# The order of the score matmuls of a head pair in a two-layer hybrid decoder: both heads interleaved, or one head after the other

## The reference, cut to what matters

```python
z = jnp.einsum('bhtd,bhsd->bhts', q_blk, k_blk) * scale      # 8 heads, d = 64
strict = s_idx < t_idx
log_beta = jax.nn.log_sigmoid(z)
log_rest = jnp.where(strict, jax.nn.log_sigmoid(-z), 0.0)
rev = lax.cumsum(log_rest, axis=3, reverse=True)
after = jnp.pad(rev[..., 1:], ((0, 0), (0, 0), (0, 0), (0, 1)))
a = jnp.exp(jnp.where(strict, log_beta + after, -jnp.inf))
outs.append(jnp.einsum('bhts,bhse->bhte', a, v_blk))
```

## Time and profile before

| what | us |
|---|---|
| median of 3 runs | 1523.18 |
| the profiled execution, whole | 1523.18 |
| its span, first to last instruction | 1521.4 |
| TensorE busy | 1476.3 (97% of the span) |
| VectorE busy | 1153.8 (76%) |
| ScalarE busy | 1007.6 (66%) |

### The profile page before, as it was taken

The page is one execution under the profiler, slowest core; times in us unless marked ns, Lnnn a source line. Parts: engine busy times, 40 slices in busy tenths (PEclk is TensorE's granted clock), DMA queues, the critical chain, the costliest instruction groups (busy, mean ns, idle before and its releaser), DMA issues.

```text
span 1521.4 us, 20635 instructions
## 1 busy us (share of the span) xinstructions
PE 1476.3 (97%) x7842; PEld 1261.1 (83%) x7842; DVE 1153.8 (76%) x872; ACT 1007.6 (66%) x834; POOL 15.5 (1%) x44
## 2 busy tenths in 40 slices
PE   5999999999999899999999999999999999999997
PEld 5897899997897788888888888888888888888775
DVE  4466544445466588899888888989889988888996
ACT  4577543344677477677777767767777776776775
POOL 3000000000000000000000000000000000000000
PEclk9999999999999899999999999999999999999999
DMA  9442555554443399999989999999999999999993
GB/s 342 146 139 97 180 169 193 178 190 156 139 139 97 111 359 372 370 330 374 374 318 373 377 319 376 371 332 362 376 355 340 377 369 322 374 375 321 348 359 128
DMA packets 185376, 430.75 MB, mean 283 GB/s; under 512 B 9048, under 2 KB 11096, under 8 KB 185328
## 3 DMA queue, kind: packets, MB, share of 16 engines
q1 hardware_dynamic: 181920, 426.27, 78.2%
q0 software_dynamic: 1184, 3.22, 0.6%
q10 hardware_dynamic: 2224, 0.59, 0.2%
HBM read 429.01 MB, written 1.05 MB: 283 GB/s over the span
## 4 chain that ended last, share of the span: by engine, by line
PE 89%; ACT 4%; DVE 3%; issue 1%; DMA 1%; ACTq 0%; DVEq 0%
PE ps L1264 81%; PE ps L1606 2%; PE ps L1636 2%; DMA wif<-in_w_in_dram 1%; ACT whi L454 1%; DVE wlo L835 1%; ACT L464 1%; PE ps L1283 1%; DVE y L857 0%; PE ps L1673 0%; PE ps L1671 0%; PE ps L1425 0%; PE ps L1410 0%; DVE y L1022 0%; ACT qkc L626 0%
## 5 line engine op out<-in xcount | busy, mean ns | idle before, releaser
L835 DVE TENSOR_TENSOR wlo<-raw,whi 128x2048 fp32r<-128x2048 f32 x405 | 926.4, 2291 | 290.3 <-ACT whi L454 289.7
L454 ACT ACTIVATE whi<-raw 128x2048 fp32r<-128x2048 f32 x405 | 776.8, 1919 | 408.0 <-PE ps L1264 406.9
L1264 PE MATMUL ps<-whi,xT_hi 128*128 128x512 f32 x1056 | 418.2, 396 | 1.5 <-DVE wlo L835 1.5
L1264 PE MATMUL ps<-wlo,xT_hi 128*128 128x512 f32 x1056 | 411.8, 390 | 0.0
L1264 PE MATMUL ps<-whi,xT_lo 128*128 128x512 f32 x1056 | 411.1, 389 | 0.0
L1264 PEld LDWEIGHTS ps<-wlo,xT_hi 128*128 128x128 f32 x1056 | 198.3, 188 | 42.5
L1264 PEld LDWEIGHTS ps<-whi,xT_hi 128*128 128x128 f32 x1056 | 198.3, 188 | 40.8 <-issue 1.7
L1264 PEld LDWEIGHTS ps<-whi,xT_lo 128*128 128x128 f32 x1056 | 198.5, 188 | 39.1
L1264 PE MATMUL ps<-whi,hid_hi 128*128 128x512 f32 (+1 forms) x536 | 210.9, 393 | 0.7 <-DVE hid_lo L1150 0.7
L1264 PE MATMUL ps<-wlo,hid_hi 128*128 128x512 f32 (+1 forms) x536 | 208.7, 389 | 0.0
L1264 PE MATMUL ps<-whi,hid_lo 128*128 128x512 f32 (+1 forms) x536 | 208.6, 389 | 0.0
(11 more groups left out here) (218 smaller groups left out, 838.4 us busy)
## 6 DMA issues: line engine op xcount, KB each, us to landing
raw<-in_moe_w_gate_dram SPq DMA_DIRECT2D x112, 1024.0 KB, 5.2
raw<-in_moe_w_up_dram SPq DMA_DIRECT2D x112, 1024.0 KB, 5.4
raw<-in_moe_w_down_dram SPq DMA_DIRECT2D x112, 1024.0 KB, 5.2
raw<-in_w_in_dram SPq DMA_DIRECT2D x28, 1024.0 KB, 5.4
raw<-in_ffn_w_gate_dram SPq DMA_DIRECT2D x10, 1024.0 KB, 5.1
raw<-in_ffn_w_up_dram SPq DMA_DIRECT2D x10, 1024.0 KB, 5.1
raw<-in_ffn_w_down_dram SPq DMA_DIRECT2D x10, 1024.0 KB, 4.9
raw<-in_w_out_dram SPq DMA_DIRECT2D x8, 1024.0 KB, 5.0
```

The source lines that it names most:

```text
L454: act.activation(whi[:, i % NSPLIT, :], raw[:, i % NRAW, :], ACT.Copy).then_inc(hi_ready, 1)
L835: dve.tensor_tensor(wlo[:, i % NSPLIT, :], raw[:, i % NRAW, :], whi[:, i % NSPLIT, :].bitcast(F32), ALU.subtract).then_inc(lo_ready, 1)
L1264: ins = pe.matmul(acc, lhs, rhs, start=start and m == 0, stop=stop and m == 2, skip_group_check=True)
```

## The change

Only `pair_scores` is changed, and in it only the order. Before, each kind of matmul is issued for both heads in turn. After, the four of one head come first, and then the four of the other. The matmuls, their operands, the wait ahead of them and the signal behind the last are the same. The lines behind move up by one.

```diff
                 def pair_scores(p):
                     if p == 0:
                         pe.wait_ge(proj_out, 7 * l + KS + 1)
-                    heads = [(slice(64 * a, 64 * a + 64), ps[:, 4 + a, :]) for a in range(2)]
-                    for s, z in heads:
+                    for a in range(2):
+                        s = slice(64 * a, 64 * a + 64)
+                        z = ps[:, 4 + a, :]
                         pe.matmul(z[:, 0:256], ksT[s, p, 0:P], qsT[s, p, :], start=True, stop=False,
                                   skip_group_check=True)
-                    for s, z in heads:
                         pe.matmul(z[:, 256:384], ksT[s, p, P:], qsT[s, p, P:], start=False,
                                   stop=False, skip_group_check=True)
-                    for s, z in heads:
                         for c in (0, 256):
                             ins = pe.matmul(z[:, c:c + P], ident_b[:], mask_s[:], start=False,
                                             stop=False, skip_group_check=True)
                     ins.then_inc(z_ps, 1)
```

## The result

The changed kernel takes 1531.41 us (median of 4 runs, 1530.53 to 1532.31), the kernel before 1522.60 us beside it (4 runs, 1520.34 to 1525.19). The ratio is 1.0058, with an interval of 1.0043 to 1.0074. Timed again, with five more runs of it beside 22 of the kernel before, the ratio is 1.0047 (1.0033 to 1.0061). The forecast, 1530.6 us or 1.0049 of the median of 1523.18, lies in both intervals, and the measured time in the forecast's range of 1527.0 to 1533.5.

A forecast was written before the change was run, and what follows sets the result against it. TensorE's chain was taken to bound the kernel. Each layer grows 4 x 0.96 - 0.16 = 3.68 us, the kernel 7.4 us: span 1528.8 us, with 1.8 us around it 1530.6 us; range 1527.0 to 1533.5.

The forecast's parts named there:

- What bounds: Whole kernel: TensorE carries 89% of the chain, the pair scores lie on it, and their added time moves everything behind.
- 0.96 us a pair: At each of 8 score pairs: added time, 0.65 us from lost overlap plus 0.31 us from switches.
- the overlap: In a score pair: no pass of one head runs beside one of the other any more, 0.65 us a pair.
- the switches: In a score pair: the array goes from 128 rows to 64 and back twice, not once, 0.31 us a pair.
- What goes back: Third pair's wait before the sums vanishes, 0.16 us a layer; fourth pair's, some 0.4 us, vanishes but gains nothing.
- Loads open: Rival, score pairs: weight load lies open at each of a lone head's four passes, 1.56 us a pair, 1535.4 us; chance 0.05.
- Only the overlap is lost: Rival, score pairs: no switch costs anything more, 0.65 us a pair, 1528.1 us; chance 0.12.
- Absorbed: Rival: the delay falls into later waits or the overlap isn't lost, no change, 1523 us; chance 0.04.
- The clock: Rival: low-clock stretches near 350 to 370 and 500 to 530 us shift into idle, 1520 us or less; chance 0.02.

The follow-up runs named there:

- same rows: Kernel before with both heads of a pair reading partitions 0 to 63, order of instructions unchanged: 1.0030 of before.
- two-switch kernel: Kernel before, heads still in turn, with the masks of the first 128 columns moved between the 256-column and the 128-column scores: 1.0013 of before.
- the kernel with the masks last: Kernel before with each head's two scores issued together, then the other head's, and the four masks behind both: 0.9994 of before.
- groups of 6: Kernel before with each head's scores as three matmuls of 128 columns, all the first head's ahead of the second's, then four masks: 1.0016 of before.
- kernel with narrow matmuls in turn: Kernel before with each head's scores as twelve matmuls of 32 columns (24 passes), the heads alternating, then the four masks: 1546.33 us, one run.
- and by head: Kernel before with twelve 32-column score matmuls (24 passes) a head, all the first head's issued before the second's: 1584.52 us, one run.

## Why the prediction was right, step by step

- **What bounds.** Right. The scores are on the chain, and each 0.1 us at a pair moves the end. The kernels order themselves by the length of a pair, with 8 pairs and 0.3 us that goes back: pairs of 1.37, 1.40, 1.71 and 2.01 us give 2.1, 2.3, 4.8 and 7.2 us; measured were 2.0, 2.4, 4.6 and 7.2 us (ratios times 1523). Each has an interval of 1.6 to 2.1 us on both sides, so the times alone don't tell the first two apart; the first timing of the changed kernel gave 8.8 us.
- **0.96 us a pair.** Measured 0.94 (2.01 against 1.07), of it the overlap 0.64 (same rows) and the switches 0.30 (masks in the middle). Both terms were forecast, 0.65 and 0.31, and each was shown alone. (By its own numbers the prediction's 0.48% is 0.49%; nothing rests on it.)
- **What goes back.** Right, in both halves. The wait ahead of the third sums is gone. The wait of the fourth pair is gone too, with the sums at 117.70 us, one step of 0.23 behind the last product, and it came back as a longer idle at the numerators (line 1397). The timelines of the changed kernel, third sums, soft step of the third pair, and numerators, to set beside the earlier trace rows:

```profile
101.37 0.28 PE L1264 MATMUL ps<-xT_hi,wlo 128*128 128x256 f32 x1
101.50 0.59 PE L1424 MATMUL ps<-scratch,tri_neg 128*128 128x256 f32 x2
...
98.89 0.94 ACT L587 ACTIVATE scratch<-scratch,ones 128x768 f32<-128x768 f32 x1
...
99.93 0.96 DVE L950 SCALAR_TENSOR_TENSOR scratch<-ps,scratch 128x768 f32<-128x768 f32 x1
...
136.28 0.62 PE L1397 MATMUL ps<-vm,scratch 128*128 128x129 f32 x2 [0.90 <-ACT om L532]
```

  The sums start one ordinary step behind the last product. The soft step ends at 100.89 and is wanted at 101.50, 0.6 us to spare (forecast 0.7). It now starts 0.1 us after ScalarE's logarithm, where VectorE came 0.8 us late before. The idle at the numerators is 0.90 us, forecast about 0.8, and it is 0.90 in the other three profiles of the changed kernel too.
- **Loads open.** Out: the steps of a lone head are 0.32, 0.22 and 0.11. The second pass's weight load is on record from 77.04 us, while the first pass, in the same rows, has been streaming since 76.93 and goes on to 77.25. So the rule that the prediction quotes from the Trainium skill, "TensorE: Matmul & The Clock Gate", that weight loads overlap only where the row group differs, doesn't hold for these passes.
- **Only the overlap is lost.** Out, by the two-switch kernel.
- **Absorbed.** Out; the idle that could have taken it up grew.
- **The clock.** As scatter of 1 or 2 us a low stretch was foreseen. That one would fall on working time inside the mixers was not: it is 1.6 us of the first profile at 61 us, and 3.1 to 3.3 us for both stretches, by the time from the first score pass (1471.5 against 1468.2 to 1468.4). Part of the first ratio of 1.0058 may be of this kind; that isn't shown.
- **What I had not seen.** For the lost overlap the prediction gave two reasons. One, that a head's 128-row masks come before the other head, holds. The other, that both heads "use the same stream of instructions in program order", so that one head after the other already means no overlap, is wrong: the kernel with the masks last shows it. By that reason a grouping by head is slower wherever the masks stand, and so the masks-last kernel was expected 4 us slower and measured no change. That the wrong reason did no harm to the forecast is luck: this change happens to put masks between the heads. That it is the masks and not the window of three passes can be read from the changed kernel: when the first head's last pass starts, at 77.58 us, only its two masks stand ahead of the other head, and yet that head starts behind them, at 78.00. So a product of all 128 rows isn't overtaken by one of 64.

## What to carry to other kernels

Two matmuls of 64 rows in different halves run at once, and it doesn't matter much which is issued first, but whether a full-depth matmul stands between them. Keep all work of the half-depth kind together, and issue it in turn or in short groups: at most three passes of one half may wait ahead of the other's. On a chain that TensorE carries, each way to 64 rows and back cost 0.30 us here, and each pass that lost its partner its whole length: 0.22 us for 256 columns in fp32, 0.11 for 128.

## What the runs showed of the hardware

- Matmuls of another row group start out of program order, over up to three waiting passes (an fp32 matmul has two). The Trainium skill, "TensorE: Matmul & The Clock Gate", section "Part 3: Packing small matmuls — row/col tiling", says that matmuls start and end in strict program order. Here the measurement decides: with the first head's four passes issued ahead, the second head started 0.01 us behind the first pass. The depth of three rests on the groups of 6 and of 24 passes. A product of all 128 rows was not overtaken.
- A switch costs 0.09 us before the first 64-row pass, 0.10 us for its weight load, which starts with the pass (both at 76.93 us) and not ahead of it, and 0.10 us on the way back. The Trainium skill's "TensorEngine Tiling (Array Packing)", section "Key Properties", says that a change of mode drains the engine and gives no time for it; these steps agree with it, as far as starts can show a drain, and give the time.
- Long runs of narrow lone passes went with a low clock, in one profile of each kernel. These are 50 to 150 us in the kernel with narrow matmuls in turn, and by head:

```profile
50.00:150.00 100.00, 98.52 (x736) 88.33 (x734) 53.30 (x70) 67.34 (x80) 0.00 (x0) 0.97 0.35 116
```

```profile
50.00:150.00 100.00, 99.42 (x608) 92.65 (x607) 40.31 (x53) 50.80 (x49) 0.00 (x0) 0.81 0.28 95
```

  The granted clock is 0.97 and 0.81 of full, though TensorE counts as busy for 98 and 99% in both. In the second the clock falls to 1.2 GHz at each of the eight pairs of the program, while TensorE streams 32 columns a pass through half of its rows. With a partner beside each pass it fell just behind three of the eight. This accounts, as an estimate, for the 38.2 us between the two kernels: 8 pairs that take 5.18 - 2.81 = 2.37 us more at full clock are 19 us. The mean clocks of the whole spans, 0.971 of 1582.7 us and 0.983 of 1544.4 us, mean 92 and 53 us at half clock, and half of the 39 us more is another 20 us.
